# Half of the expert pair weights added by GpSimd's indirect transfers into a DRAM table instead of one-hot products on TensorE

## The chip, the cores and the metric

The kernel runs on one core of a Trainium2 chip. The metric is the device time of one execution in microseconds. TensorE is written PE, its weight loads PEld, VectorE DVE, ScalarE ACT, GpSimd POOL, and SyncE, which issues nearly all transfers of the kernel before, SP.

## The reference, cut to what matters

The program is a two-layer network on 256 tokens and 256 context tokens of width 1024. The change touches only its mixture-of-experts layer, which is called three times (layer 0 on the tokens, layer 0 on the context, layer 1 on the tokens), each time for 256 tokens:

```python
def block(hb):                                   # 128 tokens
    q = (hb @ wq).reshape(tc, 8, 2, 128)
    s = einsum('thpk,hpnk->thpn', q, keys)       # 8 heads, 2 halves, 128 keys each
    s_top, i_top = top_k(s, 16)
    cand = s_top[:, :, 0, :, None] + s_top[:, :, 1, None, :]
    cid = i_top[:, :, 0, :, None] * 128 + i_top[:, :, 1, None, :]
    best, pos = top_k(cand.reshape(tc, 8, -1), 16)
    eid = take_along_axis(cid..., pos)           # 128 experts per token, of 16384
    g = softmax(best)
    act = gelu(einsum('td,thed->the', hb, u[eid]))
    return einsum('the,thed->td', g * act, v[eid])
```

An expert is a pair of keys (i, j). Of one token the 8 heads can pick the same pair, and its weights then add up.

## The kernel before, in words

It doesn't gather. `peer_experts` goes through all 128 x 128 experts densely, in two halves. In the first half (the U half) row r is one key i with its 128 experts: `products_u(r)` makes 8 x 3 matmuls of 256 columns (three products of high and low parts), ACT puts the result through gelu (`gelu`), and SP stores it in DRAM. DVE and ACT split each loaded row in a high and a low part (`split_low`, `split_high`), three rows ahead (LEAD). In the second half (the V half) `weigh(r)` multiplies the gelu row with the pair weights `wt[:, expert, :]`, a table of 128 partitions x 128 keys x 256 tokens in SBUF that is zero but for 128 pairs per token, and `products_v(r, t)` adds up the output over all rows.

That table is made in the U half. In rows 0 to 63 DVE runs `select()`, tile t = 0 (tokens 0 to 127) and then t = 1: top 16, candidate sums, best 16 and the two key numbers of each pair, cut in pieces so that about SELECT_NS = 1650 ns of it go with each row. At its end come the two softmaxes, and PE turns each tile's key numbers and weights by three transposes (`turn_selected`) that DVE copies into `table`. From row TABLE_AT = 64 on each row carries one group of TOKS = 4 tokens: for each token DVE makes two one-hot matrices (`hots`), PE multiplies them (`table_of`, two matmul records per token), which adds up duplicates, and ACT copies the group's bank into `wt` (`table_out`). 64 groups fill rows 64 to 127. GpSimd has nothing to do in the three calls.

All loads go through SP's one queue in program order. The stage in which the change puts its clearing is `mixer_ab`, which runs from 39 us on; its input weights are units u0 to u0 + 5 of a ring of three slots, and `run_ahead(sp, until)` issues the loads below `until`, each after the slot's release.

Of the kernel before, what the change touches and what calls it, by code (L numbers as in the profile page):

```python
# [54 lines left out]
SCOPES = []  # L55
STAGE_SEMS = 30
BIG_SEMS = 89

# [1487 lines left out]


def mixer_ab(nc, G):
    ws = G.ws
    u0 = ws.first["ab_in"]  # L1550
    B = Buffers()
    with scope():
        B.cat = Arena(nc, nc.sbuf_base, 4 * D * 4).take("cat", [P, 4, D], F32)
        sbuf(nc, "cat_room", [P, 4, D], F32)
        with scope():
# [87 lines left out]
            with big_stage(nc, M1_SIGNALS.split()) as (block, *sems):  # L1643
# [63 lines left out]
TOKS = 4  # L1707
GROUPS = W // TOKS
TABLE_AT = N_KEYS - GROUPS
SELECT_NS = 1650  # L1710
# [48 lines left out]
def peer_experts(nc, G, hs, queries, scores, arena, dead, wt, small, src_u, src_v, ge_dram, back, mod, end):  # L1759
# [26 lines left out]
    table, hot_i, hot_j, ge_in, aw, ah, al = small  # L1786
    if end.cols:
# [12 lines left out]
    turn_no = G.e_turn  # L1800
    G.e_turn += 1
    N = 2 * N_KEYS
    with big_stage(nc, ("high_done", "low_done", "scored", "gelu_done", "ge_stored_0", "ge_stored_1", "ge_landed_0",
# [4 lines left out]
                        "score_v", "score_s", "x_normed", "h_turned", "h_whole", "h_high", "h_low", "q_landed", "q_high",  # L1808
                        "q_low", "k_landed", "k_high", "k_low")) as (
# [4 lines left out]
            x_normed, h_turned, h_whole, h_high, h_low, q_landed, q_high, q_low, k_landed, k_high, k_low):  # L1814
        ge_stored, ge_landed = (ge_stored_0, ge_stored_1), (ge_landed_0, ge_landed_1)
# [14 lines left out]
        def expert(p):  # L1830

            return (p + N_KEYS - KEPT) % N_KEYS

        def mod_unit(r):
# [4 lines left out]
        def _(dve):  # L1839
            step = Steps(dve, sel_step)  # L1840

            def select():
                for t in range(PT):
# [6 lines left out]
                    for h0 in range(0, PEER_HEADS, LANES):  # L1850
# [13 lines left out]
                                      best[:, t, :, 0:1].broadcast_to([P, PEER_HEADS, 16]),  # L1864
                                      ALU.subtract).then_inc(shift_ready, 1)

                    pflat = pos[:, :, :].rearrange("p h m -> p (h m)")
# [31 lines left out]
                at["shift"] = at["now"]  # L1899
                for t in range(PT):  # L1900
                    dve.wait_ge(exp_ready, t + 1)
                    dve.wait_ge(sel_ready, 2 * PT + t)
# [3 lines left out]
                    yield 500  # L1906
                    step.wait()
                    dve.tensor_tensor(sel[:, t, 2, :].rearrange("p (h m) -> p h m", h=PEER_HEADS), ex[:, t, :, :],
                                      sm[:, t, :, 1:2].broadcast_to([P, PEER_HEADS, 16]), ALU.mult).then_inc(sel_ready, 1)
                    yield 300  # L1910
                for t in range(PT):
                    at[f"turn{t}"] = at["now"] + TURN_AFTER
                    yield (TURN_AFTER + 1) * SELECT_NS
                    dve.wait_ge(sel_turned, t + 1)
                    dve.tensor_copy(table[:, :, t * P:(t + 1) * P],
                                    ps[:, 3, 0:3 * P].rearrange("p (k c) -> p k c", k=3)).then_inc(table_ready, 1)
                    yield 600
                assert at[f"turn{PT - 1}"] < TABLE_AT

# [5 lines left out]
            def hots(g):  # L1925
                if g == 0:
                    dve.wait_ge(table_ready, PT)
                for k in range(g * TOKS, (g + 1) * TOKS):
# [150 lines left out]
        def _(pe):  # L2079
# [13 lines left out]
            def turn_selected(t):  # L2093
                pe.wait_ge(sel_ready, 2 * PT + t + 1)
                if t >= 1:
                    pe.wait_ge(table_ready, t)
                for k in range(3):
# [42 lines left out]
            for r in range(N_KEYS):  # L2140
                products_u(r)
                if r == 0:
                    pe.wait_ge(score_v, SCORES // 2)
                    pe.wait_ge(score_s, SCORES // 2)
                for t in range(PT):
                    if r == at[f"turn{t}"]:
                        turn_selected(t)
                u = mod_unit(r)
                if u is not None:
# [3 lines left out]
                    if u == mod.hi - 1:  # L2153
                        mod.sums(pe, u, parts_out, sums_ready)
                if r >= TABLE_AT:
                    table_of(r - TABLE_AT)
            def turn_front(q):
# [9 lines left out]
            for r in range(N_KEYS - 2):  # L2167
# [4 lines left out]
                if r == ROWS_AT:  # L2172
                    pe.wait_ge(w_out, GROUPS)
                    for n, col in enumerate(end.cols):
# [8 lines left out]
        def _(act):  # L2183
# [17 lines left out]
            def table_out(g):  # L2201
                act.wait_ge(w_ready, (g + 1) * TOKS)
                act.activation(wt[:, :, g * TOKS:(g + 1) * TOKS], ps[:, 4 + g % 4, :].rearrange("p (t j) -> p j t", t=TOKS),
                               ACT.Identity).then_inc(w_out, 1)
# [6 lines left out]
            for r in range(N_KEYS):  # L2211
                gelu(r)
                if r == N_KEYS - 1:
# [3 lines left out]
                if r == at["shift"]:  # L2217
                    for t in range(PT):
# [7 lines left out]
                if TABLE_AT < r < N_KEYS - 1:  # L2226
                    table_out(r - TABLE_AT - 1)

# [43 lines left out]
            if end.cols and front is None:  # L2272
                for t in range(PT):
                    std((PT if end.held else 0) + t)

        @block.sync
        def _(sp):
# [27 lines left out]
            load_ge(1)  # L2305
            sp.wait_ge(w_ready, W)
            for dst, src in back:
# [425 lines left out]
def peer(nc, G, layer, col, tiles, mod=None, mixed=None):  # L2733
# [9 lines left out]
    with scope():  # L2743
# [8 lines left out]
        mine = Arena(nc, own, 2 * D * 4)  # L2752
        table = mine.take("pair_table", [P, 3, W], F32)
        hot_i = mine.take("hot_i", [P, TOKS, P], F32)
# [32 lines left out]
        else:  # L2787
# [6 lines left out]
        ws.limit = None  # L2794
        peer_experts(nc, G, hs, (pq, keysT), scores, later, dead, wt, (table, hot_i, hot_j, ge_in, aw, ah, G.w_low), src_u, src_v, ge_dram,
                     [(G.x[:, ts, :], G.x_spill[:, ts, :])], mod, end)
# [2260 lines left out]
def make_shared(nc, dram):  # L5057
# [3 lines left out]
    G.ones = sbuf(nc, "ones", [P, P], F32)  # L5061
    G.iota = sbuf(nc, "iota", [P, P], F32)
    G.x = sbuf(nc, "x", [P, 4, D], F32)
    G.x_at = nc.sbuf_base - 4 * D * 4
# [23 lines left out]
    G.e_landed = [nc.alloc_semaphore(f"expert_slot{s}_landed") for s in range(E_SLOTS)]  # L5088
    G.e_turn = 0
    G.moved = nc.alloc_semaphore("rows_moved")  # L5090
    G.moves = 0
# [7 lines left out]
def load_x(nc, G):  # L5099

    with scope():
# [5 lines left out]
        with stage(nc, "x_landed", "iota_landed", "small_landed", "c_landed", "ones_set", "sc_zeroed", "silu_done", "bias_step",  # L5107
# [118 lines left out]
def constants():  # L5226
    f = np.float32
    c = {"ident": np.eye(P, dtype=f), "pick": np.tile(np.eye(PAD, dtype=f)[:, 0:2], (P // PAD, 1)), "iota": np.tile(np.arange(P, dtype=f), (P, 1))}

# [166 lines left out]
```

## Time and profile before

| | |
|---|---|
| median of 2 runs | 4057.71 us (4057.68 to 4057.74) |
| profiled execution | 4058.2 us from first to last instruction |
| PE busy | 3915.4 us (96%) |
| PEld busy | 3500.9 us (86%) |
| DVE busy | 3021.8 us (74%) |
| ACT busy | 1831.6 us (45%) |
| POOL busy | 6.5 us (0%) |
| mean granted clock of TensorE | 0.987 |
| U halves of the three calls, first to last gelu | 437 to 867, 1282 to 1746, 2390 to 2821 us |

The time outside the profiled span is not known for that execution; its span lies 0.5 us above the median of the two runs. Busy times are sums over the span, so an engine at 74% can still be full in one stage. A matmul is pipelined with the next, so its own duration (280 ns) is longer than the distance to the next one; times per row are therefore read from counts in a stretch.

### The profile page before, as it was taken

How to read it: one execution, taken by the hardware profiler on the slowest of the kernel's cores; microseconds unless marked ns; L12 is line 12 of the kernel's file. 1: busy time of each engine (PE TensorE's matmuls, PEld its weight loads, DVE VectorE, ACT ScalarE, POOL GpSimd, SP SyncE). 2: the span in 40 equal slices, each digit the busy share in tenths (PEclk: the TensorE clock that was granted, in tenths of full speed). 3: DMA queues.
4: the chain of work that ended last, by engine and by line, in shares of the span. 5: the costliest groups of instructions: out<-in, count | busy, mean ns of one | idle time of the engine just before them, and what ended most of it. 6: DMA issues, size and time to landing. Idle time of an engine off the chain costs nothing. (4 is left out here: it accounts for less than half of the span.)

```text
span 4058.2 us, 66160 instructions
## 1 busy us (share of the span) xinstructions
PE 3915.4 (96%) x25874; PEld 3500.9 (86%) x25874; DVE 3021.8 (74%) x6784; ACT 1831.6 (45%) x2929; POOL 6.5 (0%) x18
## 2 busy tenths in 40 slices
PE   7999999999999999999999899999999799998999
PEld 6768999988889999988887699999888688988798
DVE  4557797788886877788984579777888767766875
ACT  3344444443334444433444344444333535555454
POOL 0000000000000000000000000000000000000000
PEclk8999999999999999999999999999999899999999
DMA  5144575566667865567751357655666422442243
GB/s 218 60 162 152 191 227 176 169 203 239 244 228 271 315 232 169 169 237 254 258 205 57 121 169 232 193 169 182 243 244 244 158 86 91 178 175 104 78 167 146
DMA packets 121829, 752.17 MB, mean 185 GB/s; under 512 B 15728, under 2 KB 17265, under 8 KB 57265
## 3 DMA queue, kind: packets, MB, share of 16 engines
q1 hardware_dynamic: 121520, 747.93, 52.5%
q8 instruction: 209, 3.42, 0.3%
q14 instruction: 100, 0.81, 0.1%
HBM read 693.88 MB, written 54.00 MB: 184 GB/s over the span
## 5 line engine op out<-in xcount | busy, mean ns | idle before, releaser
L1922 DVE TENSOR_TENSOR expert_ring_low<-expert_ring,expert_high 128x1024 fp32r<-128x1024 f32 x768 | 935.6, 1219 | 248.0 <-ACT expert_high L2192 247.7
L2192 ACT ACTIVATE expert_high<-expert_ring 128x1024 fp32r<-128x1024 f32 x768 | 811.8, 1057 | 619.0 <-PE ps L2119 616.0
L2088 PE MATMUL ps<-peer_hT_high_peer,expert_high 128*128 128x256 f32 x3072 | 882.3, 287 | 1.2 <-DVE expert_ring_low L1922 1.0
L2089 PE MATMUL ps<-peer_hT_low,expert_high 128*128 128x256 f32 x3072 | 861.0, 280 | 0.0
L2090 PE MATMUL ps<-peer_hT_high_peer,expert_ring_low 128*128 128x256 f32 x3072 | 861.0, 280 | 0.0
L2088 PEld LDWEIGHTS ps<-peer_hT_high_peer,expert_high 128*128 128x128 f32 x3072 | 583.2, 190 | 3.3 <-DVE expert_ring_low L1922 2.4
L2089 PEld LDWEIGHTS ps<-peer_hT_low,expert_high 128*128 128x128 f32 x3072 | 584.0, 190 | 0.0
L2090 PEld LDWEIGHTS ps<-peer_hT_high_peer,expert_ring_low 128*128 128x128 f32 x3072 | 578.9, 188 | 0.0
L2119 PE MATMUL ps<-expert_high,weighted_high 128*128 128x512 f32 x1536 | 474.9, 390 | 7.4 <-DVE weighted_low L1952 7.4
L2119 PE MATMUL ps<-expert_high,weighted_low 128*128 128x512 f32 x1536 | 473.8, 390 | 0.0
L2119 PE MATMUL ps<-expert_ring_low,weighted_high 128*128 128x512 f32 x1536 | 473.4, 389 | 0.0
L2199 ACT ACTIVATE gelu_out<-ps 128x256 f32<-128x256 f32 x384 | 147.7, 385 | 707.7 <-PE ps L2090 700.9
L2119 PEld LDWEIGHTS ps<-expert_high,weighted_high 128*128 128x128 f32 x1536 | 287.7, 188 | 69.2 <-DVE weighted_low L1952 10.3
L2119 PEld LDWEIGHTS ps<-expert_high,weighted_low 128*128 128x128 f32 x1536 | 288.6, 188 | 60.2
L2119 PEld LDWEIGHTS ps<-expert_ring_low,weighted_high 128*128 128x128 f32 x1536 | 288.6, 188 | 60.0
L1932 DVE TENSOR_SCALAR hot_j<-iota,pair_table 128x128 f32<-128x128 f32 x768 | 261.1, 340 | 0.0
L2108 PE MATMUL ps<-hot_j,hot_i 128*128 128x128 f32 x1536 | 238.7, 288 | 1.0 <-DVE hot_j L1932 1.0
L2108 PEld LDWEIGHTS ps<-hot_j,hot_i 128*128 128x128 f32 x1536 | 202.7, 190 | 22.4 <-DVE hot_j L1932 16.7
L1931 DVE TENSOR_SCALAR hot_i<-iota,pair_table 128x128 f32<-128x128 f32 x768 | 214.6, 279 | 0.0
L4725 PE MATMUL ps<-hT_high,units_high 128*128 128x256 f32 x704 | 200.2, 284 | 0.0
L4725 PE MATMUL ps<-hT_low,units_high 128*128 128x256 f32 x704 | 199.4, 283 | 0.0
L4725 PE MATMUL ps<-hT_high,weight_ring_low 128*128 128x256 f32 x704 | 199.3, 283 | 0.0
(720 smaller groups left out, 6924.3 us busy)
## 6 DMA issues: line engine op xcount, KB each, us to landing
expert_ring<-in_peer_u SPq DMA_DIRECT2D x192, 1024.0 KB, 5.2
expert_ring<-in_peer_v SPq DMA_DIRECT2D x192, 1024.0 KB, 4.9
gelu_peer<-gelu_out SPq DMA_DIRECT2D x186, 256.0 KB, 5.5
gelu_in_peer<-gelu_peer SPq DMA_DIRECT2D x93, 512.0 KB, 5.7
weight_ring<-in_ffn_w_up SPq DMA_DIRECT2D x22, 2048.0 KB, 7.3
weight_ring<-in_w_in SPq DMA_DIRECT2D x14, 2048.0 KB, 7.4
weight_ring<-in_w_mod SPq DMA_DIRECT2D x12, 2048.0 KB, 8.1
weight_ring<-in_peer_wq SPq DMA_DIRECT2D x12, 2048.0 KB, 7.3
```

Source lines behind the costliest of these rows:

```text
L1922: dve.tensor_tensor(piece(low, n), piece(raw, n), high[:, n % LEAD, :].bitcast(F32), ALU.subtract).then_inc(low_done, 1)
L1931: dve.tensor_scalar(hot_i[:, k % TOKS, :], G.iota[:, :], table[:, 0, k:k + 1], None, ALU.is_equal)
L1932: dve.tensor_scalar(hot_j[:, k % TOKS, :], G.iota[:, :], table[:, 1, k:k + 1], table[:, 2, k:k + 1], ALU.is_equal, ALU.mult).then_inc(hot_ ...
L2088: pe.matmul(o, b[:, s], hT_h[:, c, :], start=(c == 0), stop=False)
L2089: pe.matmul(o, b[:, s], hT_l[:, c, :], start=False, stop=False)
L2090: mm = pe.matmul(o, lo[:, s], hT_h[:, c, :], start=False, stop=(c == DC - 1))
L2108: pe.matmul(ps[:, 4 + g % 4, k * P:(k + 1) * P], hot_i[:, k, :], hot_j[:, k, :], start=True, stop=True).then_inc(w_ready, 1)
L2119: mm = pe.matmul(ps[:, 4 + 2 * t + h, :], (ah, al)[x][:, b, t * P:(t + 1) * P], v[y][:, h * 512:(h + 1) * 512], start=(r == 0 and (x, y) = ...
L2192: act.activation(high[:, n % LEAD, :], piece(raw, n), ACT.Identity).then_inc(high_done, 1)
L2199: act.activation(ge_out[:, r % 4, :], ps[:, r % 3, 0:W], ACT.Gelu).then_inc(gelu_done, 1)
L4725: mm = pe.matmul(G.ps[:, k % 8, 0:SEQ], w[x][:, c, q * P:(q + 1) * P], self.hT[y][:, c, :], start=(c == 0 and (x, y) == PASSES[0]), stop=( ...
```

## The change

Tile 0 of each call no longer goes through one-hot matrices. STREWN = 1 tile is strewn: DVE makes for each of its 128 x 128 pairs the index of a word in a DRAM table `pairs` (16384 keys x 128 tokens x 4 bytes = 8.4 MB for a call), and GpSimd issues 128 indirect transfers, each of which adds one word per partition. It waits after every 16 of them (one head, within which a token's pairs are all different). Then it reads the table back into `wt[:, :, 0:128]` in 8 transfers of 1 MB (128 partitions x 16 keys x 512 bytes). The three tables are zeroed by 12 transfers of 2 MB from a row of zeros (512 bytes again and again), which SP issues in `mixer_ab` between the loads of its weights. Tile 1 keeps the one-hot way: 32 groups, now in every second row from 64 to 126. Each tile's softmax moves to the end of its own selection, so that ACT computes the two Exps in different rows. One small load (`rank`), one memset and a wait are added at the start. The diff's core:

```diff
+STREWN = 1
+TABLED = (PT - STREWN) * P
+GROUPS = TABLED // TOKS
+TABLE_AT = 64
+CALLS = 3
+STREWN_KEYS = 8
+CLEARS = 12
+def clear_pairs(G, sp, n):
+    k, q = divmod(n, CLEARS // CALLS)
+    rows = N_KEYS // (CLEARS // CALLS)
+    dst = pairs_by_key(G, k)[:, q * rows:(q + 1) * rows, :]
+    for t in range(STREWN):
+        sp.dma_start(dst[:, :, t * P:(t + 1) * P], G.zero[:, :].unsqueeze(1).broadcast_to([P, rows, P])).then_inc(G.pairs_cleared, 16)
...
+                    for n in range(CLEARS):
+                        ws.run_ahead(sp, u0 + 4 + n // 4)
+                        clear_pairs(G, sp, n)
...
+        def group_at(r):
+            g, odd = divmod(r - TABLE_AT, STREWN + 1)
+            return g if odd == 0 and 0 <= g < GROUPS else None
...
+                    if t < STREWN:
+                        step(dve.scalar_tensor_tensor(where[:, :], sel[:, t, 0, :], float(N_KEYS), sel[:, t, 1, :], ALU.mult,
+                                                      ALU.add))
...
+                        dve.tensor_scalar(spots[:, t, :], where[:, :], float(STREWN * P), G.rank[:, t:t + 1], ALU.mult,
+                                          ALU.add).then_inc(spots_ready, 1)
...
-                if r >= TABLE_AT - 1 and r - TABLE_AT + 1 < GROUPS:
-                    hots(r - TABLE_AT + 1)
-
-            dve.wait_ge(w_out, GROUPS)
+                if group_at(r + 1) is not None:
+                    hots(group_at(r + 1))
+
+            if GROUPS:
+                dve.wait_ge(w_out, GROUPS)
+            dve.wait_ge(G.pairs_landed, 16 * STREWN_KEYS * (turn_no + 1))
...
+        @block.gpsimd
+        def _(pool):
+            pool.wait_ge(G.pairs_cleared, 16 * CLEARS * STREWN)
+            for t in range(STREWN):
+                pool.wait_ge(spots_ready, 2 * t + 2)
+                for h in range(PEER_HEADS):
+                    for m in range(h * PEER_TOPK, (h + 1) * PEER_TOPK):
+                        pool.indirect_dma_start(pairs, bass.IndirectOffsetOnAxis(spots[:, t, m:m + 1], 0), shares[:, t, m:m + 1],
+                                                None, compute_op=ALU.add).then_inc(G.strewn, 16)
+                    pool.wait_ge(G.strewn, 16 * ((turn_no * STREWN + t) * PAIRS + (h + 1) * PEER_TOPK))
+            if TABLED:
+                pool.wait_ge(table_ready, PT - STREWN)
+            if mod is not None:
+                pool.wait_ge(mod_out, 1)
+            rows = N_KEYS // STREWN_KEYS
+            for q in range(STREWN_KEYS):
+                pool.dma_start(wt[:, q * rows:(q + 1) * rows, 0:STREWN * P],
+                               pairs_of[:, q * rows:(q + 1) * rows, :]).then_inc(G.pairs_landed, 16)
+            pool.wait_ge(G.pairs_landed, 16 * STREWN_KEYS * (turn_no + 1))
...
-            sp.wait_ge(w_ready, W)
+            if TABLED:
+                sp.wait_ge(w_ready, TABLED)
+            sp.wait_ge(G.strewn, 16 * (turn_no + 1) * STREWN * PAIRS)
...
+                sp.dma_start(G.rank[:, :], G.d["rank"]).then_inc(small_landed, 16)
...
+                dve.memset(G.zero[:, :], 0.0).then_inc(ones_set, 1)
...
-                pe.wait_ge(small_landed, 32)
+                pe.wait_ge(small_landed, 48)
```

## Rows read from the trace of the kernel before

**Rows 1.** The page: busy time of each engine, and PE's busy tenths by slice.

```profile
PE 3915.4 (96%) x25874; PEld 3500.9 (86%) x25874; DVE 3021.8 (74%) x6784; ACT 1831.6 (45%) x2929; POOL 6.5 (0%) x18
...
PE   7999999999999999999999899999999799998999
```

**Rows 2.** Windows: busy us (instructions) of PE, PEld, DVE, ACT, POOL; clock, DMA share, GB/s.

```profile
440.00:500.00 60.00, 60.00 (x512) 60.00 (x511) 59.31 (x224) 28.62 (x43) 0.00 (x0) 1.00 0.74 233
640.00:860.00 220.00, 220.00 (x1804) 214.04 (x1804) 170.66 (x507) 102.79 (x170) 0.00 (x0) 1.00 0.54 168
...
2395.00:2450.00 55.00, 55.00 (x469) 55.00 (x468) 54.34 (x213) 25.58 (x39) 0.00 (x0) 1.00 0.73 237
2600.00:2810.00 210.00, 210.00 (x1723) 204.64 (x1722) 163.06 (x486) 97.77 (x162) 0.00 (x0) 1.00 0.55 169
```

**Rows 3.** The gelu line's instructions in each call (min/median/max ns, first and last start).

```profile
L2199 ACT ACTIVATE gelu_out<-ps x128: 377/385/387, 436.8 to 867.1; 128x256 f32<-128x256 f32 x128
...
L2199 ACT ACTIVATE gelu_out<-ps x128: 384/384/388, 1281.7 to 1746.1; 128x256 f32<-128x256 f32 x128
...
L2199 ACT ACTIVATE gelu_out<-ps x128: 375/384/388, 2390.4 to 2820.5; 128x256 f32<-128x256 f32 x128
```

**Rows 4.** Waits from 620 to 870 us (total us, times, longest).

```profile
ACT gelu_out L2199 <- PE ps L2090: 134.5, 64, 3.7
...
PEld ps L2108 <- DVE hot_j L1932: 5.8, 35, 0.5
```

**Rows 5.** Groups of instructions from 640 to 860 us (busy us, mean ns, idle before).

```profile
L1932 DVE TENSOR_SCALAR hot_j<-iota,pair_table 128x128 f32<-128x128 f32 x226 | 76.7, 339 | 0.0
L2108 PE MATMUL ps<-hot_j,hot_i 128*128 128x128 f32 x456 | 70.4, 287 | 0.0
...
L1931 DVE TENSOR_SCALAR hot_i<-iota,pair_table 128x128 f32<-128x128 f32 x225 | 62.8, 279 | 0.0
```

**Rows 6.** DVE's timeline (start, us): the reduction that ends tile 0's selection, three calls.

```profile
512.50 2.27 DVE L1897 TENSOR_REDUCE selected<-one_hot 128x128 f32<-128x2048 f32 x1
...
1368.92 2.28 DVE L1897 TENSOR_REDUCE selected<-one_hot 128x128 f32<-128x2048 f32 x1
...
2466.12 2.28 DVE L1897 TENSOR_REDUCE selected<-one_hot 128x128 f32<-128x2048 f32 x1
```

**Rows 7.** ACT's timeline at the end of the first selection.

```profile
592.19 1.28 ACT L2220 ACT_TABLE_LOAD   x1
```

**Rows 8.** Page and SP's timeline: transfers with KB and median us to landing; one issue.

```profile
gelu_peer<-gelu_out SPq DMA_DIRECT2D x186, 256.0 KB, 5.5
...
c_cols<-in_c SPq DMA_DIRECT2D x1, 4.0 KB, 1.6
...
row_picker<-in_pick SPq DMA_DIRECT2D x1, 1.0 KB, 1.8
...
2.59 0.43 SPq L5117 DMA_DIRECT2D row_picker<-in_pick  x1
```

**Rows 9.** DMA view, 3.5 to 5.0 us: packets, MB; the queue's share of 16 engines.

```profile
DMA packets 305, 0.15 MB, mean 100 GB/s; under 512 B 167, under 2 KB 295, under 8 KB 295
...
q1 hardware_dynamic: 305, 0.15, 62.9%
```

**Rows 10.** SP's loads and ACT's splits in the first mixer, and its scan's mask line.

```profile
L172 SPq DMA_DIRECT2D weight_ring<-in_ab_w_in x1: 327/327/327, 91.4 to 91.4; - x1
...
115.40 0.33 SPq L172 DMA_DIRECT2D weight_ring<-in_ab_w_in  x1
118.44 0.33 SPq L1693 DMA_DIRECT2D scan_mask<-in_scan_mask  x1
...
147.90 1.04 ACT L717 ACTIVATE pieces_high<-weight_ring 128x1024 fp32r<-128x1024 f32 x1
...
194.69 1.99 ACT L717 ACTIVATE pieces_high<-weight_ring 128x1024 fp32r<-128x1024 f32 x2
...
L1176 DVE SCALAR_TENSOR_TENSOR mlstm_d<-ps,gcol,scan_mask x32: 473/616/752, 248.1 to 308.8; 128x256 f32<-128x256 f32 x16, 128x512 f32<-128x512 f32 x16
```

More of the change, by code:

```diff
@@ L55 @@
 SCOPES = []
-STAGE_SEMS = 30
-BIG_SEMS = 89
+STAGE_SEMS = 29
+BIG_SEMS = 88
 @contextmanager
@@ L1785, in peer_experts @@
         mod.slots = arena.take("mod_slots", [P, 2, UNIT], F32)
-    table, hot_i, hot_j, ge_in, aw, ah, al = small
+    spots, shares, table, hot_i, hot_j, ge_in, aw, ah, al = small
     if end.cols:
@@ L1801, in peer_experts @@
     G.e_turn += 1
+    pairs, pairs_of = G.pairs[turn_no], pairs_by_key(G, turn_no)
+    where = arena.take("spot_sums", [P, PAIRS], F32)
     N = 2 * N_KEYS
@@ L1865, in select @@
                                       ALU.subtract).then_inc(shift_ready, 1)
+                    at[f"shift{t}"] = at["now"]
                     pflat = pos[:, :, :].rearrange("p h m -> p (h m)")
@@ L1898, in select @@
                         yield 2200
-                at["shift"] = at["now"]
-                for t in range(PT):
                     dve.wait_ge(exp_ready, t + 1)
-                    dve.wait_ge(sel_ready, 2 * PT + t)
+                    dve.wait_ge(sel_ready, 2 * t + 2 + max(t - STREWN, 0))
                     step(dve.tensor_reduce(sm[:, t, :, 0], ex[:, t, :, :], AX.X, ALU.add))
+                    if t < STREWN:
+                        step(dve.scalar_tensor_tensor(where[:, :], sel[:, t, 0, :], float(N_KEYS), sel[:, t, 1, :], ALU.mult,
+                                                      ALU.add))
@@ L1904, in select @@
                     step.wait()
                     step(dve.reciprocal(sm[:, t, :, 1], sm[:, t, :, 0]))
-                    yield 500
+                    if t < STREWN:
+                        dve.tensor_scalar(spots[:, t, :], where[:, :], float(STREWN * P), G.rank[:, t:t + 1], ALU.mult,
+                                          ALU.add).then_inc(spots_ready, 1)
+                    yield 900
                     step.wait()
-                    dve.tensor_tensor(sel[:, t, 2, :].rearrange("p (h m) -> p h m", h=PEER_HEADS), ex[:, t, :, :],
-                                      sm[:, t, :, 1:2].broadcast_to([P, PEER_HEADS, 16]), ALU.mult).then_inc(sel_ready, 1)
+                    share = shares[:, t, :] if t < STREWN else sel[:, t, 2, :]
@@ L1910, in select @@
+                    dve.tensor_tensor(share.rearrange("p (h m) -> p h m", h=PEER_HEADS), ex[:, t, :, :],
+                                      sm[:, t, :, 1:2].broadcast_to([P, PEER_HEADS, 16]), ALU.mult).then_inc(
+                                          spots_ready if t < STREWN else sel_ready, 1)
                     yield 300
-                for t in range(PT):
+                for t in range(STREWN, PT):
                     at[f"turn{t}"] = at["now"] + TURN_AFTER
                     yield (TURN_AFTER + 1) * SELECT_NS
-                    dve.wait_ge(sel_turned, t + 1)
-                    dve.tensor_copy(table[:, :, t * P:(t + 1) * P],
-                                    ps[:, 3, 0:3 * P].rearrange("p (k c) -> p k c", k=3)).then_inc(table_ready, 1)
+                    dve.wait_ge(sel_turned, t - STREWN + 1)
+                    o = (t - STREWN) * P
+                    dve.tensor_copy(table[:, :, o:o + P], ps[:, 3, 0:3 * P].rearrange("p (k c) -> p k c", k=3)).then_inc(table_ready, 1)
@@ L1917, in select @@
                     yield 600
-                assert at[f"turn{PT - 1}"] < TABLE_AT
+                    assert at[f"turn{t}"] < TABLE_AT
             def split_low(n):
@@ L2093, in turn_selected @@
             def turn_selected(t):
[L2094 to L2096 removed]
+                pe.wait_ge(sel_ready, 2 * t + 2 + t - STREWN + 1)
+                if t > STREWN:
+                    pe.wait_ge(table_ready, t - STREWN)
                 for k in range(3):
@@ L2144, in _ @@
                     pe.wait_ge(score_s, SCORES // 2)
-                for t in range(PT):
+                for t in range(STREWN, PT):
                     if r == at[f"turn{t}"]:
@@ L2154, in _ @@
                         mod.sums(pe, u, parts_out, sums_ready)
-                if r >= TABLE_AT:
-                    table_of(r - TABLE_AT)
+                if group_at(r) is not None:
+                    table_of(group_at(r))
+            if mod is not None and not GROUPS:
+                pe.wait_ge(mod_out, 1)
             def turn_front(q):
@@ L2172, in _ @@
                 if r == ROWS_AT:
-                    pe.wait_ge(w_out, GROUPS)
+                    if GROUPS:
+                        pe.wait_ge(w_out, GROUPS)
                     for n, col in enumerate(end.cols):
@@ L2212, in _ @@
                 gelu(r)
-                if r == N_KEYS - 1:
+                if r == N_KEYS - 1 and group_at(r) is not None:
                     table_out(GROUPS - 2)
@@ L2216, in _ @@
                 split_high(r + LEAD)
-                if r == at["shift"]:
-                    for t in range(PT):
+                for t in range(PT):
+                    if r == at[f"shift{t}"]:
                         act.wait_ge(shift_ready, t + 1)
@@ L2225, in _ @@
                         mod.out(act, sums_ready, mod_out)
-                if TABLE_AT < r < N_KEYS - 1:
-                    table_out(r - TABLE_AT - 1)
+                if group_at(r - 1) is not None and (r < N_KEYS - 1 or group_at(r) is None):
+                    table_out(group_at(r - 1))
             def std(k):
@@ L2752, in peer @@
         mine = Arena(nc, own, 2 * D * 4)
-        table = mine.take("pair_table", [P, 3, W], F32)
+        spots = mine.take("pair_spots", [P, STREWN, PAIRS], U32)
+        shares = mine.take("pair_shares", [P, STREWN, PAIRS], F32)
+        table = mine.take("pair_table", [P, 3, max(TABLED, P)], F32)
         hot_i = mine.take("hot_i", [P, TOKS, P], F32)
@@ L2794, in peer @@
         ws.limit = None
-        peer_experts(nc, G, hs, (pq, keysT), scores, later, dead, wt, (table, hot_i, hot_j, ge_in, aw, ah, G.w_low), src_u, src_v, ge_dram,
+        peer_experts(nc, G, hs, (pq, keysT), scores, later, dead, wt, (spots, shares, table, hot_i, hot_j, ge_in, aw, ah, G.w_low), src_u, src_v, ge_dram,
                      [(G.x[:, ts, :], G.x_spill[:, ts, :])], mod, end)
@@ L5062, in make_shared @@
     G.iota = sbuf(nc, "iota", [P, P], F32)
+    G.zero = sbuf(nc, "zero_row", [P, P], F32)
+    G.rank = sbuf(nc, "own_rank", [P, STREWN], F32)
     G.x = sbuf(nc, "x", [P, 4, D], F32)
@@ L5089, in make_shared @@
     G.e_turn = 0
+    G.pairs = [nc.dram_tensor(f"pair_weights_{k}", [N_KEYS * N_KEYS * STREWN * P, 1], F32).ap() for k in range(CALLS)]
+    G.pairs_cleared = nc.alloc_semaphore("pairs_cleared")
+    G.strewn = nc.alloc_semaphore("shares_strewn")
+    G.pairs_landed = nc.alloc_semaphore("pairs_landed")
     G.moved = nc.alloc_semaphore("rows_moved")
@@ L5227, in constants @@
     f = np.float32
-    c = {"ident": np.eye(P, dtype=f), "pick": np.tile(np.eye(PAD, dtype=f)[:, 0:2], (P // PAD, 1)), "iota": np.tile(np.arange(P, dtype=f), (P, 1))}
+    c = {"rank": np.arange(STREWN * P, dtype=f).reshape(STREWN, P).T.copy(), "ident": np.eye(P, dtype=f), "pick": np.tile(np.eye(PAD, dtype=f)[:, 0:2], (P // PAD, 1)), "iota": np.tile(np.arange(P, dtype=f), (P, 1))}
     m = np.full((P, 2, QK_WIDTH), NEG, f)
```

14 lines of the change are left out of this document (8 added, 6 removed).

## The prediction

> **What bounds the kernel now.** I read the page first: PE is busy 96% of the span and in nearly every slice, GpSimd for 6.5 us in all [rows 1]. The change touches the U halves of the three expert calls and the first mixer, so I read those stretches next. In the windows PE is busy without a gap both in the rows before the table (440 to 500 us) and in the rows with it (640 to 860 us) [rows 2]. What differs is the count of records. A plain row has 24 matmuls: 512 records in 60 us are 21.3 rows, 2.81 us each (third call: 469 in 55 us, 2.81 us). A row with a table group has 24 + 8 = 32: 1804 in 220 us are 56.4 rows, 3.90 us each (third call: 1723 in 210 us, 3.90 us) [rows 2]. So a group of four tokens costs 1.09 us of PE time, and PE time is what ends last there: the waits show ACT waiting for PE in every row, 134.5 us in 64 rows, and PE's weight loads waiting for DVE's one-hots for only 5.8 us [rows 4]. DVE is at 171 of 220 us in the table rows, but at 59.3 of 60 us beside the selection [rows 2]: there it is nearly a second bound.
>
> **What it removes.** 32 of 64 groups in each call: 3 x 32 x 1.09 us = 104.4 us, all of it on the path, as long as the alternating rows still end with PE. In two such rows PE takes 2.81 + 3.90 = 6.71 us; DVE's one-hots, 76.7 + 62.8 = 139.5 us for 56.4 groups [rows 5], are 2.5 us of single durations, and with two splits of 1.2 us come to 4.9 us; ACT needs two row splits, two gelus and one copy, half of what it did, 102.8 us of 220, or less [rows 2]. Both fit. The transposes and the table copy of tile 0 go too (under 1 us a call); I count them at nothing.
>
> **What it adds on DVE and ACT.** Two 128-element operations per call for the indices, some 0.3 us each by the one-hots of the same width [rows 5], against a table copy that goes: nothing, hidden by PE, though the cover is thin beside the selection [rows 2]. If all of it showed, it would be 2 us. The second Exp in a row of its own costs ACT one more pair of table loads of 1.28 us each [rows 7], 2.6 us a call; ACT is busy 28.6 us of 60 there [rows 2] and splits three rows ahead of PE, so it costs nothing; uncovered it would be 8 us. DVE's new wait for the Exp of tile 0 has the splits of the coming rows behind it, but the Exp is asked for some 13 us of selection earlier, so it has been answered. At the start PE waits for one load more, one SP issue of 0.43 us [rows 8]: +0.4 us.
>
> **What it adds on GpSimd.** This has no row of its own, since GpSimd issues nothing now. The chain is: indices of tile 0, 128 adding transfers with 8 waits, read-back, and only then `weigh(0)`, behind which DVE holds every split of the V half, so PE waits too. Time at hand: the last reduction of tile 0 ends at 514.8, 1371.2 and 2468.4 us [rows 6]; with the softmax after it I start 3 us later. The U half ends at the last gelu, 867.1, 1746.1 and 2820.5 us [rows 3], less the 35 us saved. That leaves 314, 337 and 314 us. The price of one transfer lies between 0.43 us, an issue alone, and 5.5 us, the landing of a 256 KB store [rows 8], so between 55 and 704 us for the 128. I take 1.6 us, the landing of the 4 KB load, the nearest in size [rows 8], as if each were issued only when the one before had landed: 205 us, plus 8 waits of 1.8 us (the landing of the 1 KB load [rows 8]), 14 us. The read-back is 128 x 128 = 16384 pieces of 512 bytes, 1024 for each of the 16 engines. A 512-byte packet costs between 26 ns (the 168 GB/s at a share of 0.54 in the table rows give 19.4 GB/s for an engine [rows 2]) and 83 ns: from 3.5 to 5 us the queue used 62.9% of 16 x 1.5 us = 15.1 us for 305 packets, 10 of them of 8 KB at about 300 ns and 167 of a few bytes at about 9 ns, which leaves 10.6 us for 128 [rows 9] (the 9 ns are my estimate from the smallest packets; without it the rest only falls). I take 40 ns, because the low end has large packets in it and the high end a queue that was just starting: 41 us. Together 205 + 14 + 41 = 260 us of 314. The forecast is that it is hidden with some 54 us to spare, and the deciding price of one transfer is (314 - 14 - 41) / 128 = 2.0 us.
>
> Rows 8 have a floor of 1.6 to 1.8 us for a small transfer from issue to landing. The Trainium skill ("DMA: Bandwidth & Descriptors", Anatomy of one DMA) gives a transfer from GpSimd a fixed 2.0 us, mostly the receipt of the write; if each of the 128 paid it in turn, the sum would be 256 + 14 + 41 = 311 us, just inside the 314, but 16 are in flight at once, so its rule alone doesn't make them late.
>
> **What it adds on the DMA engines.** The read-back takes 41 us of all 16 engines within the last 100 us of the U half, where the expert loads use 0.54 to 0.74 of them [rows 2]: with a share of 0.4 more they are near full for a while, but four ring slots are ahead. I allow 1 us a call. The clears are 12 x 4096 packets, 256 for each engine, 10 us each at 40 ns: 41 us for a batch of four. They stand in SP's queue ahead of the loads issued at 91.4 us (unit u0 + 4, split by ACT at 147.9), at 115.4 us (u0 + 5, split at 194.7) and of the scan's mask at 118.4 us, first read at 248.1 us [rows 10]. From about 76 us on, the first batch ends at 117, the second at 158, the third at 199 us, each with 5 to 7 us for a weight unit between: 122, 168 and 215 us, all before they are needed. Nearest is the second: 81 + 2048 packets < 188 us puts the deciding price at 52 ns. Cost nothing; at 83 ns the unit would be some 63 us late.
>
> **The sum.** 4058.2 - 104.4 + 0.4 + 3 x 1 (engines) + 2 (DVE's thin cover) = 3959 us. Span and median differ by 0.5 us, which I leave aside: 2.4% faster, 3959 us.
>
> **Rivals.**
> (a) Transfers slower than 2.0 us. Place: `weigh(0)` of each call, PE idle. At 3 us each: 384 + 14 + 41 = 439 us, 125 us late, three times: 3959 + 375 = 4334 us, slower. It becomes a loss of 2% (4139 us) from 60 us late per call, 2.5 us each. For it speaks that a gelu store takes 5.5 us to land beside the expert stream [rows 8] and that adding means a read and a write in DRAM; against it, that 16 are in flight at once.
> (b) GpSimd works only while DVE leaves it. By the rows the one-hots are 139.5 of 220 us [rows 5], 0.63 of the table stretch; with every second group 0.37 of the time is such an operation. If GpSimd stood still in it, then of the 219 us of strewing 93 pass beside the selection and the other 126 take 200 us, and issuing the read-back 65 us: done at 882 instead of 832 us, 50 us late, 3959 + 150 = 4109 us, within 2%. No row shows GpSimd beside a busy DVE.
> The Trainium skill ("SBUF — State Buffer", SBUF: two separate sides) states this lock: while DVE runs an operation in a 2-port mode, GpSimd can't write descriptors, and a transfer of 620 ns took 3100 ns beside such a copy. By its 3.1 us the 128 transfers would take 397 us, 138 us late per call, 4373 us; no run here has shown it.
> (c) The 512-byte packets cost over 52 ns and the first mixer waits for its weights: up to 63 us for unit u0 + 5 and some 30 more for the mask, 3959 + 30 to 90, about 4020 us, within 2%. DVE held up by GpSimd beside the selection, where it has 0.7 us of 60 left [rows 2], would land there too: 10% on the selection beside the strewing is 9 us a call, 3986 us.
> (d) The change doesn't do what it says: the alternating rows don't get 1.09 us shorter because something else fills them. At half the gain it gives 4011 us. The windows speak against it, PE being full and the others not.
>
> **How the numbers follow.** Hidden as forecast 0.52 (3945 to 3976 us), (a) 0.24, of which 0.02 ends within 2%, (b) 0.13, (c) 0.08, (d) 0.03. About 2% either way is what a measurement of this kernel can tell from no change. Faster by over 2%, below 3977 us: the forecast, less a part that lands in the last microseconds, and (b) where the lateness is a few us: 0.52. Slower by over 2%: 0.23. Within: 0.25. The likeliest case's own range is 3945 to 3976 us. For 8 in 10 the range must take in (b), (c), (d) and the milder part of (a), up to 80 us late per call: 3946 to 4200 us.
>
> **What would show it.** Right: 12 clears landing before 215 us with no new wait of L717 or L1176; U halves 35 us shorter; matmul records of the one-hot line halved, 768; POOL's transfers at or under 2 us apart, the last of the read-back before the last gelu; the first `weigh` with no wait for POOL's queue. Wrong: a hole of PE at each turn from the U to the V half, with the first V products waiting on `weighted` and that on a transfer into `expert_weights` (a, b); between these two, transfers that are slow already beside the selection (a) or only beside the one-hots (b); ACT waiting for a weight unit between 120 and 250 us (c).

## The result and the profile after

The changed kernel took 4098.02 us (median of 2 runs, 4093.09 to 4102.96) against 4057.71 us before: ratio 1.0097, 95% interval 1.0066 to 1.0127. It is slower by 1%, where 2.4% faster was forecast. The profiled execution spans 4091.3 us, 33 us more than before.

From the page of the changed kernel: its head with busy time, its costliest line on GpSimd, and the one-hot products (busy us, mean ns of one; idle before):

```profile
PE 3881.9 (95%) x25097; PEld 3431.8 (84%) x25097; DVE 2853.7 (70%) x6020; ACT 1790.5 (44%) x2839; POOL 720.8 (18%) x426
...
L2328 POOL DMA_INDIRECT pair_weights<-pair_shares,pair_spots x384 | 686.3, 1787 | 1918.5 <-DVE pair_shares L1946 1687.2
...
L2149 PE MATMUL ps<-hot_j,hot_i 128*128 128x128 f32 x768 | 165.6, 322 | 54.5 <-DVE hot_j L1971 54.1
```

The one-hot records are halved, as the change says (768 instead of 1536), but PE now sits idle 54.5 us ahead of them, waiting for DVE's one-hots. The gelu line in the three calls, against [rows 3]:

```profile
L2243 ACT ACTIVATE gelu_out<-ps x128: 375/383/386, 438.3 to 877.1; 128x256 f32<-128x256 f32 x128
...
L2243 ACT ACTIVATE gelu_out<-ps x128: 375/383/387, 1294.0 to 1763.1; 128x256 f32<-128x256 f32 x128
...
L2243 ACT ACTIVATE gelu_out<-ps x128: 376/383/386, 2409.2 to 2848.1; 128x256 f32<-128x256 f32 x128
```

The U halves take 438.8, 469.1 and 438.9 us where they took 430.3, 464.4 and 430.1. They should have lost 35 us each and have grown by 5 to 9. That is 22 of the 33 us; the start adds 1.5 us, and what follows the U halves adds 2.3, 1.8 and 5.5 us. The windows, against [rows 2] (a pair is a row without a table group and the row with one that follows it; 24 + 32 = 56 matmul records):

```profile
640.00:860.00 220.00, 203.58 (x1547) 188.60 (x1546) 120.46 (x280) 86.38 (x138) 144.62 (x87) 1.00 0.72 190
...
640.00:760.00 120.00, 111.69 (x850) 103.39 (x848) 65.24 (x153) 47.29 (x76) 90.17 (x53) 1.00 0.67 167
```

PE is no longer full. It has 16 us of holes at full clock in the longer window, and the engine that the change relieved, DVE, has fallen from 171 to 120 us: neither is full, so each waits for another in a ring. A pair takes 56 / 850 x 120 = 7.91 us, where two rows took 7.80 us before. DVE, ACT, GpSimd and the one-hot products on PE in the changed kernel's timeline around one pair of rows (start, us; idle before and its releaser):

```profile
733.59 1.05 ACT L2236 ACTIVATE expert_high<-expert_ring 128x1024 fp32r<-128x1024 f32 x1
734.54 0.59 ACT L2248 ACTIVATE expert_weights<-ps 128x512 f32<-128x512 f32 x1
...
734.68 1.23 DVE L1961 TENSOR_TENSOR expert_ring_low<-expert_ring,expert_high 128x1024 fp32r<-128x1024 f32 x1 [3.64 <-ACT expert_high L2236]
...
735.82 0.38 DVE L1970 TENSOR_SCALAR hot_i<-iota,pair_table 128x128 f32<-128x128 f32 x1
736.01 0.34 DVE L1971 TENSOR_SCALAR hot_j<-iota,pair_table 128x128 f32<-128x128 f32 x1
...
736.48 1.54 POOL L2328 DMA_INDIRECT pair_weights<-pair_shares,pair_spots  x1 [0.30 <-issue]
736.50 0.85 PE L2149 MATMUL ps<-hot_j,hot_i 128*128 128x128 f32 x4 [0.40 <-DVE hot_j L1971]
...
736.92 0.64 DVE L1971 TENSOR_SCALAR hot_j<-iota,pair_table 128x128 f32<-128x128 f32 x1
737.17 0.45 DVE L1970 TENSOR_SCALAR hot_i<-iota,pair_table 128x128 f32<-128x128 f32 x1
...
737.62 0.81 PE L2149 MATMUL ps<-hot_j,hot_i 128*128 128x128 f32 x4 [0.27 <-DVE hot_j L1971]
737.80 1.21 DVE L1961 TENSOR_TENSOR expert_ring_low<-expert_ring,expert_high 128x1024 fp32r<-128x1024 f32 x1
...
738.33 2.11 POOL L2328 DMA_INDIRECT pair_weights<-pair_shares,pair_spots  x1 [0.30 <-issue]
```

DVE stands idle for 3.64 us, for the high part of a row three ahead, before it may make the one-hots that PE needs next: in its program the split comes first. The high part waits in its turn for the slot that PE frees at the end of the row before. In the kernel before, DVE's wait for the high part was 0.69 us, and the one-hots followed the split in the same way, 0.45 us from token to token:

```profile
700.22 1.23 DVE L1922 TENSOR_TENSOR expert_ring_low<-expert_ring,expert_high 128x1024 fp32r<-128x1024 f32 x1 [0.69 <-ACT expert_high L2192]
701.36 0.28 DVE L1931 TENSOR_SCALAR hot_i<-iota,pair_table 128x128 f32<-128x128 f32 x1
...
701.82 0.28 DVE L1931 TENSOR_SCALAR hot_i<-iota,pair_table 128x128 f32<-128x128 f32 x1
```

Two of the one-hot operations in the changed kernel also take 0.64 and 0.45 us instead of 0.34 and 0.28, beside a transfer of GpSimd, and the transfer beside the next split takes 2.11 us instead of 1.54.

GpSimd's lines in the first call (min/median/max ns, first and last start), and the last issues in its timeline:

```profile
L2328 POOL DMA_INDIRECT pair_weights<-pair_shares,pair_spots x128: 1543/1557/3045, 522.8 to 825.4; - x128
...
829.36 8.15 POOL L2337 DMA_DIRECT2D expert_weights<-pair_weights  x7 [1.81 <-DMA pair_weights<-pair_shares,pair_spots]
872.15 1.16 POOL L2337 DMA_DIRECT2D expert_weights<-pair_weights  x1 [34.63 <-issue]
```

Strewing lasts from 523 to 829 us, 306 us, and the read-back's eighth transfer is issued only at 872 us, after a wait of 34.6 us. The U half ends at 877. So GpSimd is done just when the slow U half is: had the rows been as fast as forecast (end at 832 us), PE would have had to wait for GpSimd. Two limits lie on top of each other, and the experiments have to take them apart.

### The profile page after: what moved, and what is told of

The parts are those of the page before. It is cut to its first block and busy times, and to the rows that moved or that the text cites. A ratio compares the mean times of both kernels' runs of the same rounds, so it can differ in the third digit from the quotient of the medians.

```text
span 4091.3 us, 64086 instructions
## 1 busy us (share of the span) xinstructions
PE 3881.9 (95%) x25097; PEld 3431.8 (84%) x25097; DVE 2853.7 (70%) x6020; ACT 1790.5 (44%) x2839; POOL 720.8 (18%) x426
## 3 DMA queue, kind: packets, MB, share of 16 engines
q1 hardware_dynamic: 171008, 773.10, 53.6%
## 5 line engine op out<-in xcount | busy, mean ns | idle before, releaser
L2328 POOL DMA_INDIRECT pair_weights<-pair_shares,pair_spots x384 | 686.3, 1787 | 1918.5 <-DVE pair_shares L1946 1687.2
L2149 PE MATMUL ps<-hot_j,hot_i 128*128 128x128 f32 x768 | 165.6, 322 | 54.5 <-DVE hot_j L1971 54.1
L2149 PEld LDWEIGHTS ps<-hot_j,hot_i 128*128 128x128 f32 x768 | 114.2, 188 | 107.1 <-issue 52.4
L1989 DVE CAST weighted_high<-weighted 128x256 fp32r<-128x256 f32 x384 | 112.6, 293 | 118.8 <-PE ps L2160 117.6
```

Of the source, the lines that this page charges most:

```text
L1989: dve.tensor_copy(ah[:, r % 2, :], aw[:, :]).then_inc(ah_done, 1)
L2149: pe.matmul(ps[:, 4 + g % 4, k * P:(k + 1) * P], hot_i[:, k, :], hot_j[:, k, :], start=True, stop=True).then_inc(w_ready, 1)
L2328: pool.indirect_dma_start(pairs, bass.IndirectOffsetOnAxis(spots[:, t, m:m + 1], 0), shares[:, t, m:m + 1], None, compute_op=ALU.add).then ...
```

## The experiments

The seven kernels below ran in two lots, each compared with runs of the kernel before on the same chip: e1 to e4 in the first, e5 to e7 in the second.

**One-hots a row earlier** (e1_early). On DVE the one-hots of a group are issued a row before:

```diff
-                if group_at(r + 1) is not None:
-                    hots(group_at(r + 1))
+                if r < N_KEYS - 2 and group_at(r + 2) is not None:
+                    hots(group_at(r + 2))
```

> The changed kernel with the one-hot matrices of a group issued on DVE one row earlier. Order theory: in the changed kernel the one-hots of a group stand on DVE behind the split of the row three ahead, which is ready some 2.7 us after PE ends the row before, while PE reaches the table after 2.8 us of row, so the four tokens' one-hots (0.45 us each) end 0.9 us or more late per group; issued a row earlier they are ready, and two rows take 6.7 to 7.0 us instead of 7.9. But the table of tile 0 is read back only at about 879 us in the first call, so the gain of about 35 us per U half turns into a hole of PE of 35 to 45 us ahead of the V half: time 4080 to 4105 us. Port theory (GpSimd's transfers stretch DVE's one-hots, and that alone holds PE): two rows stay near 7.9 us, no hole, 4091 us.

Measured: 4105.74 us, ratio 1.0115 (1.0098 to 1.0132). The gelu line of its first call, its windows in the table rows, behind the U half and after the hole there, and the wait that ends the hole:

```profile
L2243 ACT ACTIVATE gelu_out<-ps x128: 373/385/387, 436.7 to 830.4; 128x256 f32<-128x256 f32 x128
...
640.00:760.00 120.00, 120.00 (x1028) 120.00 (x1028) 79.85 (x187) 58.33 (x93) 91.31 (x48) 1.00 0.76 199
...
850.00:870.00 20.00, 0.00 (x0) 0.00 (x0) 0.00 (x0) 0.00 (x0) 5.57 (x5) 0.50 1.02 301
...
890.00:910.00 20.00, 20.00 (x83) 16.40 (x82) 14.33 (x27) 7.00 (x7) 0.00 (x0) 0.92 0.41 141
...
DVE weighted L1983 <- DMA expert_weights<-pair_weights: 56.6, 1, 56.6
```

In 120 us PE makes 1028 matmuls: a pair takes 6.54 us, against 7.91 us in the changed kernel (850 in the same window). PE is full, while GpSimd is busy for 91 of the 120 us. The U half is 393.7 us, 36.6 us shorter than in the kernel before; and all of it, with 20 us more, comes back as one wait of 56.6 us for the read-back, in which PE does nothing and its granted clock is 0.50, the lower of its two levels (1.2 GHz). The other two calls have the same wait, 49.7 and 53.6 us. Both halves of the order theory hold in kind: the rows are fast and the hole appears, though it is longer than the 35 to 45 us expected, and the time is 0.7 us above the expected range. The port theory, by which the two rows should have stayed at 7.9 us, falls.

**One head of eight strewn** (e3_one_head: the inner loop over 16 transfers runs for h = 0 only, and the waits count 16), with the one-hots where they are, and **both edits together** (e4_early_one_head).

> The changed kernel with the indirect transfers of one head of eight only (16 of 128 per call); the pair weights of the other seven heads of tile 0 are left out. Order theory: PE still waits 0.9 us per group, two rows take about 7.6 us, U halves of about 425 us instead of 438.8, time about 4045 us. Port theory: without GpSimd two rows take 6.7 us, U halves of about 397 us, time about 3970 us.

> Both edits: one-hots a row earlier, and one head of eight strewn (the pair weights of the other seven heads of tile 0 are left out). Order theory together with a late GpSimd as the second limit: the forecast's saving appears, U halves of about 398 us, no hole, time about 3970 us. If the one-hot products were not the cost, the time stays near that of the kernel with one head alone.

Measured: 4085.56 us (ratio 1.0059, 1.0042 to 1.0075) and 3964.45 us (0.9773, 0.9756 to 0.9789). The same window in the two, and in the first one DVE's wait in front of a split:

```profile
640.00:760.00 120.00, 114.14 (x866) 105.32 (x866) 62.90 (x152) 48.78 (x78) 1.15 (x1) 1.00 0.63 201
...
728.52 1.22 DVE L1961 TENSOR_TENSOR expert_ring_low<-expert_ring,expert_high 128x1024 fp32r<-128x1024 f32 x1 [3.64 <-ACT expert_high L2236]
```

```profile
640.00:760.00 120.00, 119.70 (x1018) 119.12 (x1018) 77.36 (x181) 56.59 (x90) 1.16 (x1) 1.00 0.71 229
```

With GpSimd nearly silent and late one-hots, DVE still waits 3.64 us in a pair, and two rows still take 56 / 866 x 120 = 7.76 us. So of the 1.37 us that a pair loses against 6.54, the order makes 1.22 us and GpSimd's hold on DVE 0.15 us. With early one-hots GpSimd's silence gains a pair nothing: 56 / 1018 x 120 = 6.60 us here, 6.54 us in e1_early. The time of e3_one_head fell far less than I had expected of the order theory (4085.56 instead of 4045 us; its first U half is 436.8 instead of 425 us): I had put the order's stall at 0.9 us, and in this kernel the read-back comes early, issued from 613 to 658 us, beside fast rows, and costs about 5 us up to row 64 (the first U half with early one-hots is 399.1 us, and 393.7 us with the whole strewing). With both edits the time is 3964 us, 5 us from the forecast. It leaves seven eighths of the strewing out; e6_halves below reaches the same time with all of it.

**Early one-hots and a read-back piece by piece** (e2_early_piecewise), the whole computation. GpSimd reads back the piece of the last 16 keys first, since the V half begins there, waits for each piece, and DVE waits only for the piece that its next row reads (the one-hots are moved as in e1_early):

```diff
+            for k in range(STREWN_KEYS):
+                q = (k + STREWN_KEYS - 1) % STREWN_KEYS
...
+                pool.wait_ge(G.pairs_landed, 16 * (STREWN_KEYS * turn_no + k + 1))
...
+                if r == 0 or expert(r) % rows == 0:
+                    k = (expert(r) // rows + 1) % STREWN_KEYS
+                    dve.wait_ge(G.pairs_landed, 16 * (STREWN_KEYS * turn_no + (k if k or r < KEPT else STREWN_KEYS - 1) + 1))
```

> The whole computation: one-hots a row earlier, and the read-back in the order of the V rows (piece 7 first), GpSimd waiting for each piece and DVE waiting only for the piece that its next row reads. If both limits are as read, U halves of about 400 to 405 us and a seam of a few us, since strewing ends at 829 us and the first piece lands some 7 us later: time 3975 to 4000 us. If GpSimd's transfers slow down further when DVE's one-hots move, or the read-back beside the V loads holds the V rows up, over 4020 us.

Measured: 4022.07 us, ratio 0.9907 (0.9889 to 0.9924). It beats the kernel before and the changed one, but not by what was expected (3975 to 4000 us). Its wait behind the first U half, and GpSimd's timeline there:

```profile
DVE weighted L1987 <- DMA expert_weights<-pair_weights: 27.5, 1, 27.5
```

```profile
830.61 1.56 POOL L2331 DMA_INDIRECT pair_weights<-pair_shares,pair_spots  x1 [4.71 <-issue]
832.48 1.57 POOL L2331 DMA_INDIRECT pair_weights<-pair_shares,pair_spots  x1 [0.30 <-issue]
...
843.62 1.56 POOL L2331 DMA_INDIRECT pair_weights<-pair_shares,pair_spots  x1 [0.30 <-issue]
846.89 1.23 POOL L2341 DMA_DIRECT2D expert_weights<-pair_weights  x1 [1.71 <-DMA pair_weights<-pair_shares,pair_spots]
```

Half of the hole has gone, from 56.6 to 27.5 us: the seven further pieces are no longer waited for. What remains is the strewing itself: it now ends at 847 instead of 829 us, 17 us behind the U half, and the first piece lands some 10 us later. I had taken over 829 us from a kernel whose rows were slower; beside the fast rows a transfer takes 1.91 us in the mean of the first call instead of 1.81. That is what the other case of the expectation said, and the time lies over its 4020 us.

**Piecewise read-back alone** (e5_piecewise), one-hots late as in the changed kernel.

> The changed kernel with only the read-back waited for piece by piece; one-hots stay where they are. If the two limits hide each other (U halves long enough that GpSimd is done just in time), this alone gives nothing: within 10 us of the changed kernel, 4085 to 4100 us. If GpSimd's end was what held the changed kernel, it gains 30 us or more.

Measured: 4088.56 us, ratio 1.0068 (1.0053 to 1.0084), 10 us under the changed kernel's median, at the expected edge. The two intervals overlap (1.0066 to 1.0127 for the changed kernel), so even these 10 us are not clear of the noise. As long as the rows are slow, a faster end of GpSimd's chain is worth next to nothing.

**The table rows side by side** (e7_rows_together): as e5_piecewise, DVE's order untouched, but the 32 groups in rows 96 to 127.

```diff
-TABLE_AT = 64
+TABLE_AT = N_KEYS - GROUPS
...
-            g, odd = divmod(r - TABLE_AT, STREWN + 1)
+            g, odd = r - TABLE_AT, 0
```

> As the kernel with piecewise waits, but the 32 groups of one-hot products stand in rows 96 to 127, one in each, instead of every second row from 64; nothing else is moved. Order theory: with a table in the row before, PE reaches the next one 3.9 us after the row's products, and the one-hots are ready, so the stall of about 1.2 us per group is gone without touching DVE's order: plain rows of 2.8 us, table rows of 3.9, U halves of about 395 us, time within 15 us of the kernel with early one-hots and piecewise waits (4022 us). If GpSimd's hold on DVE were the cause, the stall would stay where it is, since the transfers run beside these rows as well: time 4085 us or more.

Measured: 4011.34 us, ratio 0.9879 (0.9864 to 0.9894). Its windows in plain rows and in table rows:

```profile
640.00:700.00 60.00, 60.00 (x512) 60.00 (x511) 25.75 (x21) 28.63 (x44) 45.76 (x21) 1.00 0.81 233
760.00:820.00 60.00, 60.00 (x486) 57.65 (x485) 47.24 (x138) 27.28 (x45) 44.16 (x26) 1.00 0.68 174
```

Plain rows take 60 / (512 / 24) = 2.81 us as in [rows 2], table rows 60 / (486 / 32) = 3.95 us, and PE is full in both, beside the same transfers of GpSimd. Nothing of the work differs from e5_piecewise, only which rows carry it, and 77 us are gone. So what costs is that the row before a table row was a short, plain one, and not GpSimd. The U half is 401.3 us instead of the 395 expected, and of the hole at the turn 11.6 us of waiting for the read-back are left in the first call.

**Tile 0 selected in two halves** (e6_halves): e2_early_piecewise with the selection of tile 0 cut into heads 0 to 3 and 4 to 7, each with its own Exp, indices and shares; the rest is as it was. Of the diff, which rewrites the whole selection:

```diff
+PARTS = [((0, 4), (4, 8)) if t < STREWN else ((0, 8),) for t in range(PT)]
...
+                        if h % 4 == 0:
+                            pool.wait_ge(spots_ready, 2 * (2 * t + h // 4 + 1))
```

> The whole computation. The kernel with early one-hots and piecewise waits (4022 us), with tile 0 selected in two halves of four heads, so that GpSimd can begin after the first half, some 35 us earlier. If GpSimd's chain of 324 us from the first index to the last sum is what leaves the hole of 28 us per call, the hole closes to a few us: 3945 to 3970 us. If the hole comes from something else at the turn (the read-back's landing, the clock), it stays above 4000 us. The extra small operations on DVE, which is nearly full there, may cost 1 to 3 us a call.

Measured: 3964.31 us, ratio 0.9760 (0.9747 to 0.9773). GpSimd's lines in its first call, its gelu line, and the wait at the turn:

```profile
L2339 POOL DMA_INDIRECT pair_weights<-pair_shares,pair_spots x128: 1537/1620/3044, 484.1 to 797.6; - x128
...
L2349 POOL DMA_DIRECT2D expert_weights<-pair_weights x8: 1148/1148/1232, 802.1 to 867.2; - x8
...
L2252 ACT ACTIVATE gelu_out<-ps x128: 377/385/388, 438.9 to 834.4; 128x256 f32<-128x256 f32 x128
...
PE ps L2169 <- DVE weighted_low L2001: 3.2, 1, 3.2
```

Strewing takes 318 us still, but begins at 484 instead of 523 us and ends at 802, 32 us ahead of the U half's end. The hole is 3.2 us, and the last four pieces are issued behind the turn without PE seeing it. The U half is 395.5 us, 1.8 us longer than with one selection; a third Exp and the further small operations lie in it, and were not told apart. This is the change with its saving kept: 2.4% faster than before.

## Why the prediction was wrong, point by point

- **What bounds the kernel, and the price of a group.** Right. PE was full, and a pair of rows with one group less takes 6.54 us when nothing else stands in the way; I had 6.71. The 56 records cost 117 ns each, as in a plain row, so the 1.09 us of a group had some 0.15 us of waiting in them. Before, two rows took 7.80 us: the saving is 32 x (7.80 - 6.54), some 40 us per call, not 35 (96 x 1.09 is 104.6, not the 104.4 of the sum, which changes nothing).
- **"As long as the alternating rows still end with PE" and "Both fit".** This is the step that failed, and the one that decided. I added up busy times per pair of rows (DVE 4.9 of 6.7 us) and took what fits in sum to fit in time. But the one-hots have a place in DVE's program behind the split of the row three ahead, which isn't free before PE ends the row before. From the timeline of the kernel before one could have worked it out: from PE's end of a row 1.4 us on ACT and 1.2 on DVE, then four times 0.45 us, 4.4 us in all, while PE arrives at the table after 2.81 us where the row before had none and after 3.90 where it had one. Before, the rows were long enough to cover it. The change took the cover away from every row that has a table. It costs 1.22 us per group (e3_one_head against e1_early), 39 us per call, about all of the saving; e7_rows_together shows it from the other side. This reckoning gives 0.9 of the 1.22 us; where the rest goes was not found.
- **Rival (d), the alternating rows filled by something else.** This is the rival that came true, at a chance of 0.03. I had set it aside because PE was full in the windows and the others were not, which is the same error: what filled the rows was a wait in program order and not a full engine. In its own terms the gain was not half but none: a pair takes 7.91 us, where two rows took 7.80.
- **GpSimd's price.** The form of the sum was right, my price too low. I had 219 us for the strewing; it took 306. The transfers come at least 1.86 us apart (1.56 + 0.30, in e2_early_piecewise while DVE stands idle) where I had 1.6, 238 us for 128. The rest is the waits, 25 us where I had 14, other gaps of some 14 us in which nothing shows, and some 30 us in longer transfers beside a busy DVE. The read-back took some 50 us instead of 41 in the changed kernel (829 to 872 us, and the landing of the last). So the chain was 356 us of the 314 at hand, as rival (a) has it; in its terms (356 - 14 - 41) / 128 = 2.35 us per transfer, above the deciding 2.0 and a little below the 2.5 that it needed to lose 2%. "Hidden with some 54 us to spare" was therefore wrong too. In the changed kernel it hardly shows, since the first limit hides it; in e1_early it makes a hole of 57 us.
- **Rival (b), GpSimd held up by DVE.** Right in kind, smaller in size, and not by the operations named. The hold exists in both directions (transfers of up to 3.7 us instead of 1.56, one-hots of 0.64 instead of 0.34). PE loses 0.15 us per pair of rows by it. GpSimd's own chain loses the some 30 us above, against the 50 us of the rival; they are hidden in the changed kernel and part of the hole in e1_early. (The rival's terms, 93 + 200 + 65 us after 517.8, end at 876 and not at 882 us, 44 us late and 4091 us in all.) It is not the one-hots that stretch a transfer but the splits: in the changed kernel the 73 transfers beside which DVE did nothing took 1.54 to 1.57 us and the 86 beside a split alone 2.03 us in the mean, while the 23 beside one-hots alone in e7_rows_together took at most 1.64 us.
The Trainium skill's rule of the shared port ("SBUF — State Buffer", SBUF: two separate sides) agrees in direction: one of the two holds the other up. Its transfer of 3.1 us instead of 0.62, five times as long, is not what these runs show, where the longest is 3.7 us and the mean 1.79 us in the changed kernel.
- **The second Exp and the indices at nothing.** Wrong, at the size that the prediction gave for the case without cover (8 us). The first 64 rows of the first and the third call went from 183 to 187 us, those of the second did not grow: some 8 us in all. The loss comes at the two Exps, not beside the strewing, and e3_one_head with its 16 transfers has it too. At an Exp ACT stands still between its table loads, waiting for DVE:

```profile
490.55 1.28 ACT L2265 ACT_TABLE_LOAD   x1
493.79 0.31 ACT L2265 ACTIVATE best_exp<-best_shift 128x128 f32<-128x128 f32 x1 [1.96 <-DVE best_shift L1895]
494.12 1.28 ACT L2243 ACT_TABLE_LOAD   x1
```

  In the kernel before, both Exps stood together and ACT did not wait for them.
- **The clears.** Right, at the low end of the price: a 2 MB clear issued every 6.6 us, 4096 packets over 16 engines, so 26 ns a packet, and the mask's line starts at 249.7 instead of 248.1 us, which is the start's 1.5 us (0.4 in the forecast). What I had not seen is that they hold SP itself:

```profile
68.84 25.39 SPq L1562 DMA_DIRECT2D pair_weights<-zero_row  x4
94.28 6.81 SPq L172 DMA_DIRECT2D weight_ring<-in_ab_w_in  x1
101.12 26.45 SPq L1562 DMA_DIRECT2D pair_weights<-zero_row  x4
127.62 7.21 SPq L172 DMA_DIRECT2D weight_ring<-in_ab_w_in  x1
134.87 26.30 SPq L1562 DMA_DIRECT2D pair_weights<-zero_row  x4
161.29 7.12 SPq L1713 DMA_DIRECT2D scan_mask<-in_scan_mask  x1
```

The mask was issued at 161 instead of 118 us; it had the time.

Of the 33 us by which the changed kernel is longer, some 14 lie in the rows with tables, 8 at the Exps, and 11 at the start and behind the U halves. The forecast of 3959 us was wrong for this program; 3964 us are reached when the two chains are moved out of the way (e6_halves). That this is so near is partly luck: in e6_halves the groups saved 121 us and not 104, and what was added cost some 25 us and not 5. The range reached to 4200 us, but the rivals that come near 4098 us, (a) and (b), do so by a hole at the turn; that the measured time lies in the range, by another mechanism, is luck. Open is what three gaps of 2 to 6.5 us in each call's strewing are, in which GpSimd waits for nothing that the profile shows. They always stand at the same places, behind the 60th, 113th and 120th transfer of a call, in the changed kernel and in the five others that strew the whole tile, however the rows are laid out; why there is not known. Open is also how much of the strewing the eight waits really cost: leaving them out would let sums of the same pair meet, so it was not tried. Of the last 5.5 us behind the third U half, 4.1 lie in the V half, 2.8 of these at the turn, where PE's hole is 4.7 instead of 1.9 us.

## What to carry to other kernels

When work is taken from some rows of a pipeline, check not only that each engine's sum of busy time still fits but that each hand-over does: follow the longest chain from the event that frees a buffer to the instruction that needs it, through every engine's program order, and compare it with the new, shorter row. What was covered by the removed work may need to be issued one row earlier. And when an idle engine is given a long serial chain, see when its first input exists and in which order its output is consumed: starting at the first half of the input and handing over piece by piece were worth 58 us (e6_halves against e2_early_piecewise) and some 80 us (that against e1_early) here, without making the chain itself shorter. Handing over piece by piece was worth next to nothing as long as the rows were slow (e5_piecewise).

## What the runs showed that I had not expected

- Of GpSimd's transfers of 2048 pieces of 512 bytes, seven are issued within 8.2 us and the eighth waits 34.6 us (35.0 and 34.9 in the other calls). It looks like a limit on what is taken in ahead; no run tested it.
- SP's issue of a transfer with 4096 pieces of 512 bytes holds SP for about 6.6 us, against 0.33 to 0.43 us for one with long pieces [rows 8], and what is queued behind it too.
- A hole of 50 to 57 us in PE's work costs more than itself: the granted clock was 0.50 in it and 0.92 in the 20 us in which PE worked again, with 83 matmuls where the next 20 us have 90 (e1_early, 890 to 910 us).
